# Stick-breaking attention layer on one core: a new split of the projection stream and a new order on ScalarE

## The chip, the cores and the metric

The kernel runs on one core of one Trainium2 chip. The metric is the device time of one execution in microseconds (us), lower is better.

## What is computed

The layer is one residual block, `x + mixer(rmsnorm(x))`, followed by a final RMSNorm, for 2048 tokens of 1024 channels in float32. The mixer projects to q, k, v and a gate g (`w_in`, 1024 x 4096), has 16 heads of 64 channels, multiplies the heads' output by silu(g) and projects back. Its attention is strictly causal:

```python
z = einsum(q[t], k[s]) / sqrt(64)
log_rem = where(s < t, log_sigmoid(-z), 0)
after = cumsum(log_rem, reversed over s) - log_rem
w = where(s < t, exp(log_sigmoid(z) + after), 0)
o = w @ v
```

## The kernel before

Tokens are reversed, so that the reversed cumulative sum becomes a forward scan. Every float32 operand is split into a high and a low part, and a product is three matmuls (high x high, high x low, low x high).

**Stages.** First v is projected and the input scaled (to about 200 us). Then comes the attention stage (about 232 to 1466 us), into which the projections of q, k and g are woven. Last come the gated output projection and the final norm (1466 us to the end).

**The attention stage** goes over heads h, chunks c of 512 query tokens and blocks j = c..3 of 512 key positions. One (h, c, j) is a *slot*: 160 slots, 10 in a head, in the order c0j0, c0j1, c0j2, c0j3, c1j1, ..., c3j3. A slot with j = c is *diagonal* and starts a chunk. A slot has two *halves* (320 halves) of two steps each (`STEPS`, L137). In each half

- TensorE turns two blocks of scanned rows into one pair of PSUM banks (`turns`, L890: up to 16 transposes of 64 rows), multiplies the turned rows of the half before with the value differences into the bank `o_ps` (`weigh_beside`, L969, twice: once for the lower and once for the upper 64 rows), and makes the scores of two steps of two slots further on (L865).
- ScalarE copies the turned rows to `r_turned_hi` (`hi`, L1182), takes the sigmoid of the two new scores (`stick`, L1175), and stores with its own DMA queue.
- VectorE subtracts to get `r_turned_lo` (`lo`, L1402) and runs two scans (`scan`, L1390).

There is one pair of turn banks only: `turns` of a half waits until `lo` of the half before is done (L893). There is one `o_ps` bank: the first weighing of a chunk waits until ScalarE has copied the finished chunk out (`empty`, L1186, wait at L953). Within `weigh_beside` the second weighing of a half waits until the last matmul of the first has finished (L976, L978), since both add into the same bank.

**Row halves.** All these matmuls use 64 of the 128 rows of the array. A matmul on the upper 64 rows and one on the lower 64 rows can run beside each other. While one row half weighs, the other makes scores.

**The stream.** The projections of q, k and g are 178 groups of 24 matmuls for each row half (`group_half`, L908; 256 columns each; 4272 for the upper rows and as many for the lower). They are the filling of the attention stage. `UPTO` (L169) says how many upper ones are to be done by the end of each half: 12 more in a half of a diagonal slot, 15 more in any other (`QUOTA`, L156). The lower rows stay 30 (`BEHIND`) behind. `weigh_beside` first lets the row half that has less to do take some stream matmuls; then `group_pairs` (L933) issues upper and lower ones in turn. Its last call in a half has `share` 1 and issues what is left, first uppers, then lowers.

```python
both = min(left(h, 0), left(h, 1)) // share
for _ in range(both):
    group_half(0)
    group_half(1)
```

**Finished groups.** When a group is complete, ScalarE copies its bank to `made` (`made_high`, L1135), VectorE makes the low part (`made_low`, L1377), and ScalarE issues the store of the high part (L1152) and of the low part (`store_low`, L1158), which waits for VectorE. ScalarE's order in a half (L1287 to L1316) is: copy and high store of finished groups, `hi`, `store_low`, two sigmoids, then in a diagonal slot `empty` (first half) or the two stores of the chunk (second half, L1192).

**The planner.** Which half finishes a group (`FINISHED`, L170) follows from `UPTO`, and from that the steps at which weights are loaded (`LOAD_W`, L176) and at which the last pieces are prepared (L202 to L213).

## Time and profile before

| | us |
|---|---|
| median of three runs | 1629.98 |
| lowest, highest | 1627.0, 1630.36 |
| the profiled execution, its own time | 1635.98 |
| its span, first to last instruction | 1634.2 |
| TensorE busy (matmuls) | 1573.5 |
| VectorE busy | 1282.4 |
| ScalarE busy | 883.9 |
| mean granted TensorE clock, share of full speed | 0.992 |

PE is TensorE (PEld its weight loads), DVE is VectorE, ACT is ScalarE, POOL is GpSimd; a q behind a name is the engine's sequencer, where it issues DMAs. A matmul's duration in the profile includes its way through the array: the distance between the starts of two that follow each other is shorter than a duration. A row of a timeline has start, length, engine, line, operation, output<-input, shapes and count, and in brackets the idle time before it with what ended it.

### The profile page before, as it was taken

How to read it: one execution, taken by the hardware profiler on the slowest of the kernel's cores; microseconds unless marked ns; L12 is line 12 of the kernel's file. 1: busy time of each engine (PE TensorE's matmuls, PEld its weight loads, DVE VectorE, ACT ScalarE, POOL GpSimd, SP SyncE). 2: the span in 40 equal slices, each digit the busy share in tenths (PEclk: the TensorE clock that was granted, in tenths of full speed). 3: DMA queues.
4: the chain of work that ended last, by engine and by line, in shares of the span. 5: the costliest groups of instructions: out<-in, count | busy, mean ns of one | idle time of the engine just before them, and what ended most of it. 6: DMA issues, size and time to landing. Idle time of an engine off the chain costs nothing. (4 is left out here: it accounts for less than half of the span.)

```text
span 1634.2 us, 46030 instructions
## 1 busy us (share of the span) xinstructions
PE 1573.5 (96%) x19314; PEld 1459.2 (89%) x19314; DVE 1282.4 (78%) x1525; ACT 883.9 (54%) x1558; POOL 414.0 (25%) x520
## 2 busy tenths in 40 slices
PE   9999989999999999999999999999999998999998
PEld 7888889899999999998999899999999998868887
DVE  4535338888888888897888898889889897967873
ACT  6635336566655666665655566656655665842221
POOL 0022033224323243323332433324422340000000
PEclk9999989999999999999999999999999999999999
DMA  9968643434334252434343343524253436779621
GB/s 306 274 180 272 183 142 109 124 111 124 124 105 122 88 156 76 140 94 129 105 121 115 111 118 102 152 73 140 81 157 87 123 102 204 249 248 318 203 103 65
DMA packets 205933, 238.57 MB, mean 146 GB/s; under 512 B 54560, under 2 KB 162080, under 8 KB 205728
## 3 DMA queue, kind: packets, MB, share of 16 engines
q1 hardware_dynamic: 113344, 160.30, 32.0%
q10 hardware_dynamic: 92384, 75.33, 15.2%
q8 instruction: 154, 2.52, 0.7%
q14 instruction: 51, 0.42, 0.1%
HBM read 155.78 MB, written 79.76 MB: 144 GB/s over the span
## 5 line engine op out<-in xcount | busy, mean ns | idle before, releaser
L957 PE MATMUL o_ps<-r_turned_hi,dv_head 64*128 64x512 f32 (+3 forms) x1280 | 481.4, 380 | 21.6 <-ACT o_stage L1190 19.7
L1400 DVE TENSOR_TENSOR_SCAN u<-u,u 128x512 f32<-128x512 f32 x384 | 485.5, 1304 | 0.0
L1179 ACT ACTIVATE u<-z_ps 128x512 f32<-128x512 f32 (+3 forms) x640 | 330.9, 533 | 265.1 <-PE z_ps L880 177.0
L923 PE MATMUL group_ps<-hT_hi,w_hi 64*128 64x256 f32 x1888 | 453.6, 281 | 2.9 <-DVE made L1384 2.0
L957 PE MATMUL o_ps<-r_turned_lo,dv_head 64*128 64x512 f32 (+3 forms) x1280 | 454.1, 365 | 0.0
L923 PE MATMUL group_ps<-hT_hi,w_lo 64*128 64x256 f32 x1888 | 448.8, 280 | 0.0
L923 PE MATMUL group_ps<-hT_lo,w_hi 64*128 64x256 f32 x1888 | 447.6, 279 | 0.0
L1404 DVE TENSOR_TENSOR r_turned_lo<-turn_ps,r_turned_hi 128x1024 fp32r<-128x1024 f32 (+1 forms) x320 | 337.5, 1055 | 130.6 <-ACT r_turned_hi L1184 129.8
L1184 ACT ACTIVATE r_turned_hi<-turn_ps 128x1024 fp32r<-128x1024 f32 (+1 forms) x320 | 287.5, 899 | 172.6 <-PE turn_ps L902 149.6
L923 PEld LDWEIGHTS group_ps<-hT_hi,w_hi 64*128 64x128 f32 x1888 | 318.5, 186 | 8.1 <-DVE made L1384 2.8
L923 PEld LDWEIGHTS group_ps<-hT_lo,w_hi 64*128 64x128 f32 x1888 | 314.4, 186 | 2.1
L923 PEld LDWEIGHTS group_ps<-hT_hi,w_lo 64*128 64x128 f32 x1888 | 314.0, 186 | 1.0
L957 PEld LDWEIGHTS o_ps<-r_turned_hi,dv_head 64*128 64x128 f32 x1280 | 240.8, 188 | 36.3 <-issue 31.1
L923 PE MATMUL z_ps<-hT_hi,w_hi 64*128 64x256 f32 x960 | 270.8, 282 | 0.7 <-DVE made L1384 0.4
L923 PE MATMUL z_ps<-hT_hi,w_lo 64*128 64x256 f32 x960 | 269.5, 281 | 0.0
L923 PE MATMUL z_ps<-hT_lo,w_hi 64*128 64x256 f32 x960 | 268.6, 280 | 0.0
L880 PE MATMUL z_ps<-k_hi_twice,q_hi 64*128 64x512 f32 (+3 forms) x640 | 260.7, 409 | 3.8 <-ACT u L1179 2.9
L957 PEld LDWEIGHTS o_ps<-r_turned_lo,dv_head 64*128 64x128 f32 x1280 | 240.0, 187 | 4.3
L756 POOL TENSOR_SCALAR w_raw<-w_raw,a_norm_col 128x128 f32<-128x128 f32 x192 | 165.3, 877 | 266.2 <-DMA w_raw<-in_w_qkg 266.2
L880 PE MATMUL z_ps<-k_hi_twice,q_lo 64*128 64x512 f32 (+3 forms) x640 | 232.2, 364 | 0.0
L880 PE MATMUL z_ps<-k_lo_twice,q_hi 64*128 64x512 f32 (+3 forms) x640 | 231.7, 364 | 0.0
L902 PE MATMUL turn_ps<-ident,u 64*128 64x64 f32 x4352 | 206.2, 224 | 23.4 <-DVE r_turned_lo L1404 22.7
(180 smaller groups left out, 3253.2 us busy)
## 6 DMA issues: line engine op xcount, KB each, us to landing
qk_hi_cols<-made ACTq DMA_DIRECT2D x128, 128.0 KB, 2.4
qk_lo_cols<-made ACTq DMA_DIRECT2D x128, 128.0 KB, 2.5
k_hi_twice<-qk_hi_cols SPq DMA_DIRECT2D x128, 128.0 KB, 3.2
k_lo_twice<-qk_lo_cols SPq DMA_DIRECT2D x128, 128.0 KB, 3.6
x_T<-in_xT SPq DMA_DIRECT2D x29, 512.0 KB, 6.5
w_raw<-in_w_qkg SPq DMA_DIRECT2D x24, 512.0 KB, 4.0
x_rows<-in_x SPq DMA_DIRECT2D x16, 512.0 KB, 4.8
v_rows<-v_stage ACTq DMA_DIRECT2D x32, 256.0 KB
```

The lines of the kernel that those rows point to most:

```text
L756: last = nc.gpsimd.tensor_scalar(w_raw[t % 2][:, k, :], w_raw[t % 2][:, k, :], norm_col[:, k:k + 1], None, ALU.mult)
L880: last = nc.tensor.matmul(score_bank(m), a[c % 2][rows, tau], b[rows, sig], start=(n == 0), stop=(n == 2))
L902: last = nc.tensor.transpose(turn_ps[:, half, at:at + HALF], u_t[m // CB % RU][t][rows, r * P - lo:(r + 1) * P - lo], ident[rows, rows])
L923: last = nc.tensor.matmul(bank_of(g)[:, 0:GW], a[t % 2][rows, k, :], b[rows, c // 2, k, cols], start=(n == 0 and not low), stop=(n == QPM ...
L957: last = nc.tensor.matmul(o_ps[:, 0:w], dv_head[rows, j * CB + sigma_block(m), :], turned_part[p % 2][rows, here], start=first, stop=(end ...
L1179: nc.scalar.activation(u_t[(m // CB) % RU][r][:, 0:w], score_bank(m), ACT.Sigmoid, scale=-Z_SCALE).then_inc(s_u, 1)
L1184: nc.scalar.activation(by_halves(rt_hi[p % 2][:], p), turned(p), ACT.Copy).then_inc(s_hi, 1)
L1400: nc.vector.tensor_tensor_scan(u, u, other, start, ALU.mult, op).then_inc(s_r, 1)
L1404: nc.vector.tensor_tensor(by_halves(rt_lo[p % 2][:], p), turned(p), by_halves(as_f32(rt_hi[p % 2][:]), p), ALU.subtract).then_inc(s_lo, 1)
```

## The change

The quotas 12 and 15 go. `limits` works out for each half how long VectorE's work would outlast TensorE's, averages this over three halves, adds an equal amount to each so that the sum fits, and caps a half at 16. The lower rows may come no nearer to the upper ones than 26. `group_pairs` takes a largest count in place of the share; in the second half of a diagonal slot it is also called ahead of the first weighing. ScalarE issues `store_low` behind both sigmoids, and `empty` comes between them. Three helper functions only move up in the file.

```diff
-QUOTA = {True: 12, False: 15}
+SWITCH = 4
+STREAM_HALVES = 2 * (NU - 4)
+MOST = 16
+SCAN_COLUMN, LOW_COLUMN = 5.8, 2.3
+
+def spare_columns(h):
+    s, p = h // 2, h
+    low = blocks_of_pair(p) * P
+    scans = [CH - score_cols(m) for m in range(PAIR * h + LEAD_SCORES - PAIR, PAIR * h + LEAD_SCORES) if m < NS]
+    scored = [CH - score_cols(m) for m in range(PAIR * h + LEAD_SCORES, PAIR * h + LEAD_SCORES + PAIR) if m < NS]
+    weighed = 2 * blocks_of_pair(max(p - 1, 0)) * P
+    return SCAN_COLUMN * sum(scans) + LOW_COLUMN * low - low - weighed - 1.5 * sum(scored)
 
 def limits():
-    upto = [0]
+    each = [spare_columns(h) / (GW + 10) for h in range(STREAM_HALVES)]
+    spare = [sum(each[max(h - 1, 0):h + 2]) / len(each[max(h - 1, 0):h + 2]) for h in range(STREAM_HALVES)]
+    more = (STREAM + BEHIND - sum(spare)) / STREAM_HALVES
+    upto, total = [0], 0.0
     for h in range(2 * NU):
-        _, c, j, _ = STEPS[CB * (h // 2)]
-        upto.append(min(upto[-1] + QUOTA[c == j], STREAM + BEHIND))
+        total += spare[h] + more if h < STREAM_HALVES else 0
+        upto.append(max(upto[-1], min(round(total), STREAM + BEHIND, upto[-1] + MOST)))
     return upto
...
                 def left(h, low):
                     limit = UPTO[h + 1] - BEHIND if low else UPTO[h + 1]
+                    if low and made_so_far[0] < STREAM:
+                        limit = min(limit, made_so_far[0] - QPM - 2)
                     return max(0, min(limit, STREAM) - made_so_far[low])
 
-                def group_pairs(h, share):
-                    both = min(left(h, 0), left(h, 1)) // share
-                    for _ in range(both):
+                def group_pairs(h, most=QPM):
+                    for _ in range(min(left(h, 0), left(h, 1), most)):
                         group_half(0)
                         group_half(1)
-                    if share == 1:
+                    if most == QPM:
                         for low in range(2):
                             for _ in range(left(h, low)):
                                 group_half(low)
...
-                    group_pairs(2 * s, 2)
+                    group_pairs(2 * s, SWITCH)
                     weigh_beside(2 * s - 1, 0, ahead + 1, 2 * s)
-                    group_pairs(2 * s, 1)
+                    group_pairs(2 * s)
...
                     turns(2 * s + 1)
+                    if diagonal(s):
+                        group_pairs(2 * s + 1, SWITCH)
                     weigh_beside(2 * s, 0, ahead + 2, 2 * s + 1)
-                    group_pairs(2 * s + 1, 2)
+                    group_pairs(2 * s + 1, SWITCH)
                     weigh_beside(2 * s, 1, ahead + 3, 2 * s + 1)
-                    group_pairs(2 * s + 1, 1)
+                    group_pairs(2 * s + 1)
...
                         if inside(s):
                             hi(h)
+                        if inside(s + LEAD):
+                            stick(first + LEAD_SCORES)
+                        if ended is not None and part == 0:
+                            empty(ended)
+                        if inside(s + LEAD):
+                            stick(first + LEAD_SCORES + 1)
                         for g in finished(h - 1):
                             store_low(g)
-                        if inside(s + LEAD):
-                            stick(first + LEAD_SCORES)
-                            stick(first + LEAD_SCORES + 1)
...
-                        if ended is not None and part == 0:
-                            empty(ended)
```

## Rows read from the trace of the kernel before

**Rows 1.** The page: busy time and share of the span of each engine.
```profile
PE 1573.5 (96%) x19314; PEld 1459.2 (89%) x19314; DVE 1282.4 (78%) x1525; ACT 883.9 (54%) x1558; POOL 414.0 (25%) x520
```

**Rows 2.** Who waited for whom, TensorE, 238 to 1466 us: total, times, longest.
```profile
PE turn_ps L902 <- DVE r_turned_lo L1404: 22.7, 41, 2.0
PE o_ps L957 <- ACT o_stage L1190: 19.7, 53, 3.7
```

**Rows 3.** Timeline of TensorE around 802 us: stream matmuls of both row halves.
```profile
802.04 0.27 PE L923 MATMUL group_ps<-hT_hi,w_hi 64*128 64x256 f32 x1
802.15 0.27 PE L923 MATMUL group_ps<-hT_lo,w_hi 64*128 64x256 f32 x1
802.18 0.28 PE L923 MATMUL z_ps<-hT_hi,w_hi 64*128 64x256 f32 x1
...
802.30 0.28 PE L923 MATMUL z_ps<-hT_lo,w_hi 64*128 64x256 f32 x1
```

**Rows 4.** Timeline of TensorE around 1420 us: stream matmuls of the lower half alone.
```profile
1419.71 0.28 PE L923 MATMUL z_ps<-hT_hi,w_lo 64*128 64x256 f32 x1
...
1420.78 0.28 PE L923 MATMUL z_ps<-hT_hi,w_lo 64*128 64x256 f32 x1
```

**Rows 5.** Timeline of TensorE at 248 us: upper stream matmuls alone, then transposes.
```profile
248.29 0.28 PE L923 MATMUL group_ps<-hT_hi,w_lo 64*128 64x256 f32 x1
248.41 0.28 PE L923 MATMUL group_ps<-hT_hi,w_hi 64*128 64x256 f32 x1
248.42 0.28 PE L902 MATMUL turn_ps<-ident,u 64*128 64x64 f32 x1
248.53 0.28 PE L923 MATMUL group_ps<-hT_lo,w_hi 64*128 64x256 f32 x1
248.54 0.27 PE L902 MATMUL turn_ps<-ident,u 64*128 64x64 f32 x1
248.66 0.28 PE L923 MATMUL group_ps<-hT_hi,w_lo 64*128 64x256 f32 x1
248.66 0.46 PE L902 MATMUL turn_ps<-ident,u 64*128 64x64 f32 x5
```

**Rows 6.** Timeline of TensorE at 1423 us: the end of one weighing and the next.
```profile
1423.08 0.39 PE L957 MATMUL o_ps<-r_turned_lo,dv_head 64*128 64x512 f32 x1
1423.10 0.28 PE L923 MATMUL z_ps<-hT_hi,w_hi 64*128 64x256 f32 x1
1423.22 0.28 PE L923 MATMUL z_ps<-hT_lo,w_hi 64*128 64x256 f32 x1
1423.61 0.46 PE L957 MATMUL o_ps<-r_turned_hi,dv_head 64*128 64x512 f32 x1
```

**Rows 7.** Timeline of ScalarE, first half of a slot that starts a chunk.
```profile
840.90 0.60 ACT L1179 ACTIVATE u<-z_ps 128x512 f32<-128x512 f32 x1 [0.86 <-PE z_ps L880]
841.39 0.59 ACT L1190 ACTIVATE o_stage<-o_ps 128x512 f32<-128x512 f32 x1
```

**Rows 8.** The same moment on TensorE.
```profile
841.47 0.39 PE L902 MATMUL turn_ps<-ident,u 64*128 64x64 f32 x6
842.13 0.47 PE L957 MATMUL o_ps<-r_turned_hi,dv_head 64*128 64x512 f32 x1 [0.27 <-ACT o_stage L1190]
```

**Rows 9.** ScalarE's waits that the moved operations touch, 238 to 1466 us.
```profile
ACT u L1179 <- DVE made L1386: 43.1, 52, 1.9
ACT u L1179 <- DVE made L1384: 37.6, 40, 1.8
ACT o_stage L1190 <- DMA o_lo_cols<-o_stage: 4.0, 3, 3.1
```

**Rows 10.** The low store's issue on ScalarE's queue: ns min/median/max, first and last start.
```profile
L1161 ACTq DMA_DIRECT2D qk_lo_cols<-made x128: 326/327/1886, 188.8 to 1262.7; - x128
L1161 ACTq DMA_DIRECT2D gate_cols<-made x64: 321/326/364, 483.1 to 1427.5; - x64
```

**Rows 11.** Timeline of ScalarE between a chunk's stores and the next turned rows.
```profile
851.47 1.65 ACTq L1196 DMA_DIRECT2D o_hi_cols<-o_stage  x1
851.78 0.59 ACT L1179 ACTIVATE u<-z_ps 128x512 f32<-128x512 f32 x1
853.15 0.61 ACTq L1197 DMA_DIRECT2D o_lo_cols<-o_stage  x1
853.87 0.42 ACT L1127 ACTIVATE dv_head<-v_here 128x256 fp32r<-128x256 f32 x1 [1.49 <-issue]
854.19 1.01 ACT L1184 ACTIVATE r_turned_hi<-turn_ps 128x1024 fp32r<-128x1024 f32 x1
```

**Rows 12.** Timeline of VectorE over one half of a non-diagonal slot.
```profile
858.74 0.40 DVE L1386 TENSOR_TENSOR made<-group_ps,made 128x256 fp32r<-128x256 f32 x1
859.05 1.22 DVE L1404 TENSOR_TENSOR r_turned_lo<-turn_ps,r_turned_hi 128x1024 fp32r<-128x1024 f32 x1
860.18 2.46 DVE L1400 TENSOR_TENSOR_SCAN u<-u,u 128x512 f32<-128x512 f32 x2
```

More of the change, by code:

```diff
@@ L155, with score_cols, sigma_block, turn_width @@
 BEHIND = 30
-QUOTA = {True: 12, False: 15}
-STREAM = (NG - FIRST) * QPM
+SWITCH = 4
+def score_cols(m):
+    _, c, j, r = STEPS[m]
+    return r * P if j == c else 0
+def sigma_block(m):
+    _, c, j, r = STEPS[m]
+    return CB - 1 - r if j == c else r
+def turn_width(m):
+    _, c, j, _ = STEPS[m]
+    return (sigma_block(m) + 1) * P if j == c else CH
+def blocks_of_pair(p):
+    return (turn_width(PAIR * p) + turn_width(PAIR * p + 1)) // P
+STREAM = (NG - FIRST) * QPM
+STREAM_HALVES = 2 * (NU - 4)
[8 more added lines that the diff above has]
+    return SCAN_COLUMN * sum(scans) + LOW_COLUMN * low - low - weighed - 1.5 * sum(scored)
 def limits():
-    upto = [0]
+    each = [spare_columns(h) / (GW + 10) for h in range(STREAM_HALVES)]
+    spare = [sum(each[max(h - 1, 0):h + 2]) / len(each[max(h - 1, 0):h + 2]) for h in range(STREAM_HALVES)]
+    more = (STREAM + BEHIND - sum(spare)) / STREAM_HALVES
+    upto, total = [0], 0.0
     for h in range(2 * NU):
-        _, c, j, _ = STEPS[CB * (h // 2)]
-        upto.append(min(upto[-1] + QUOTA[c == j], STREAM + BEHIND))
+        total += spare[h] + more if h < STREAM_HALVES else 0
+        upto.append(max(upto[-1], min(round(total), STREAM + BEHIND, upto[-1] + MOST)))
     return upto
@@ L213 @@
 LAST_SLOT = LAST_PIECE_STEP // CB
-def score_cols(m):
-    _, c, j, r = STEPS[m]
-    return r * P if j == c else 0
-def sigma_block(m):
-    _, c, j, r = STEPS[m]
-    return CB - 1 - r if j == c else r
-def turn_width(m):
-    _, c, j, _ = STEPS[m]
-    return (sigma_block(m) + 1) * P if j == c else CH
 def chunk_end(u):
@@ L239, in blocks_before @@
     return turn_width(m - 1) // P if m % PAIR else 0
-def blocks_of_pair(p):
-    return (turn_width(PAIR * p) + turn_width(PAIR * p + 1)) // P
 def inside(u):
@@ L499, in lows_stored, with diagonal @@
                 eng.wait_ge(s_gst[parity], low_stores(g, parity))
+        def diagonal(u):
+            return STEPS[CB * u][1] == STEPS[CB * u][2]
         def score_bank(m):
```

## The prediction

> **What bounds the kernel.** I read the page's busy line first: TensorE is busy 96% of the span, VectorE 78%, ScalarE 54% [rows 1]. So the change can gain only what TensorE waits, or lose by making TensorE's own work longer. Next come TensorE's waits over the attention stage [rows 2]: 22.7 us in 41 waits of transposes for VectorE's `r_turned_lo`, and 19.7 us in 53 waits of a chunk's first weighing for ScalarE's copy of `o_ps`. No other wait there is above 2 us. A stream matmul lasts 0.28 us in the profile but the next on its row half starts 0.118 us after it, so a wait hides about another 0.16 us behind the last matmul's tail: 41 x 0.16 = 6.6 and 53 x 0.16 = 8.5 us. The two waits are worth about 29 and 28 us.
>
> The third view is the timeline of TensorE, for what a stream matmul costs. Where uppers and lowers are issued in turn, each row half starts one about every 0.12 us, both halves at once (802.04, 802.15 on one bank, 802.18, 802.30 on the other) [rows 3]. Where only one row half has work, the distance is the same: from 1419.71 to 1420.78 there are ten starts, so nine distances of 0.118 [rows 4]. **A single costs as much as a pair.** So what matters is in which order uppers and lowers are issued.
>
> **Part 1, the order of the stream.** The new `left` holds the lower rows 26 behind the uppers. At the end of a half they are 30 behind. When the last `group_pairs` of a half starts, the uppers still have the rest of the half's quota to go, so `left(h, 1)` is at most 4 or so, and `range(min(...))` is worked out once, before the loop. It issues those few pairs; what is left then follows in the two loops below: all uppers, then all lowers. Before the change `min(left, left)` gave the full rest, and at most two were left single in the steady halves. I counted this out of the code for all 320 halves: after the change 258 halves end in a run of n uppers followed by at least n lowers (n from 1 to 12, most often 8), together 1271 pairs that are no longer issued in turn. Before there are none.
>
> What this costs depends on how far one row half may run ahead of the other. The trace shows it where the first halves have uppers only [rows 5]. All transposes stand behind the stream matmuls in the program. Yet one starts at 248.42, right behind the stream matmul of 248.41, with those of 248.53 and 248.66 still to come, and the first transpose, of the upper rows, as well: it has passed three matmuls. The next start at 248.54 and 248.66, in step with the stream, while transposes otherwise follow each other closer (six of them in 0.39 us) [rows 8]. So a matmul passes three that wait on the other row half and no more. Then the lowers of a run of n start with the (n-3)rd upper, (n-4) x 0.118 us later than in turn. Over the 258 halves the sum of n-4, where positive, is 381: 381 x 0.118 = **+45 us**.
>
> The bounds: nothing, if the limit of three is not general (0), and 1013 x 0.118 = 120 us if a lower could start only with the last upper. I take 45, since rows 5 are the only place with exactly this pattern.
>
> The Trainium skill ("TensorE: Matmul & The Clock Gate", Step-by-step: what each phase is for) says that only weight loads are pulled ahead and the matmuls themselves stay in program order, in a window 64 deep. The trace disagrees: the transpose at 248.42 started before two stream matmuls that precede it. By that rule the term would be the 120 us.
>
> **Part 2, fewer pairs between the two weighings.** The second weighing of a half waits for the end of the first (L976, L978). In the tail, where few stream matmuls are left, the last weighing matmul starts at 1423.08 and the next weighing at 1423.61: 0.54 us is the least distance [rows 6]. Before, 5 to 9 stream matmuls of the same row half lie between them in the steady halves, at least 0.22 + 4 x 0.118 = 0.7 us: no wait. After, `SWITCH` and the limit of 26 leave fewer. By the count, in the second halves of c0j2, c1j2, c2j2 and c2j3 (61 halves) none is left for the row half that weighed: it has 0.22 us of work and idles 0.31 us. In those of c0j1, c0j3 and c1j3 (47 halves) two are left: 0.22 + 0.24, idle 0.08. 61 x 0.31 + 47 x 0.08 = **+23 us**. The bounds are 0, if the other row half's work covers it, and 108 x 0.31 = 33 us.
>
> **Part 3, the copy of `o_ps` earlier, and four pairs ahead of the chunk's first weighing.** Before, the copy stands behind the second sigmoid: that starts at 840.90, the copy at 841.39, and the weighing at 842.13 after 0.27 us idle [rows 7, 8]. Put between the sigmoids, the copy comes 0.49 us earlier, and four pairs (0.47 us) move ahead of the weighing. Together 0.96 us against a mean wait of 19.7 / 53 + 0.16 = 0.53 us. It takes away all but the long ones that come from the landing of the chunk before (4.0 us in 3) [rows 9]: 28 - 4 = **-24 us**. The work moved is the same, so nothing is added. The second sigmoid starts some 0.5 us later; its scan is a half later. What is late next is the copy of turned rows, `hi`: it still starts behind the same sum of ScalarE's work.
>
> **Part 4, the new shares.** Per half they become about 16 in c0j0 to c0j2, 15 to 16 in c1j1 and c1j2, 11 to 12 in c0j3, c1j3 and c3j3, and 8 in the second half of c2j3, in place of 12 and 15. The stream's sum is unchanged, so the shares cost nothing by themselves; they decide which waits go. The waits of the transposes lie in the first halves of c0j0, c0j1, c0j2, c1j1, c1j2 and c2j3. There the chain copy 1.01, `lo` 1.22 [rows 11, 12] starts late, since ScalarE has two stores and `dv_hi` ahead of it [rows 11]. All but c2j3 get longer by parts 1 and 4 (0.4 to 0.9 us a slot), more than their mean wait. I take two thirds of 29: **-20 us**. Bounds: 0 and -29. In return VectorE needs 1.22 + 2.46 and 0.40 where a group ends, 3.7 to 4.1 us [rows 12], in the second halves of c0j3 and c1j3, where TensorE's work shrinks to about 3.5 us; the next half is long and takes it up. Free.
>
> **Part 5, `store_low` behind the sigmoids.** The sigmoids waited 43.1 + 37.6 us for VectorE's low part [rows 9], but TensorE hardly waited for a sigmoid (not in rows 2), so that by itself gives nothing. The issue of 0.33 us [rows 10], 178 times, moves from time in which ScalarE waited to the stretch right before the next `hi`. In c2j3, which does not get longer, and for the chunk stores' halves it delays `lo`: about half of 16 x 0.33 = 2.6, **+3 us**; bounds 0 and 20 (a third of the 178, each in full). The transfers start under 2 us later and are needed slots later. POOL and SP queues see only shifts of one or two halves in the loads (`LOAD_W` follows `FINISHED`): free, covered by a lag of 9 steps; if that cover went, a group's first matmul would wait.
>
> **Sum.** 45 + 23 - 24 - 20 + 3 = **+27 us**, against the profiled execution's own 1635.98: 1663. This execution is 6.0 us above the median of the runs, so the forecast is 1657 us. I lean a little to the gain's side, since restarts after each of the 94 waits of before also fall away, and say **1654**.
>
> **The rivals.**
> - *Runs cost nothing, the waits go* (faster). Place: the join of uppers and lowers. If the lowers may pass eight or more waiting uppers, part 1 is 0 and the sum is -18; without part 2 as well it is -41. It decides from a reach of seven on. That gives 1612 (1589 to 1612), chance 0.17. For it: the sequencer runs far ahead, and nothing in steady halves before shows a limit. Against it: rows 5.
> - *In balance.* Reach of five to six, 20 us less than forecast and a little more of the waits: 1627 to 1633. Chance 0.08.
> - *The waits stay* (parts 1, 2 and 5 in full, half of 3 and 4): 1630 + 71 - 22 = 1679, with part 5 at its upper end 1690. For it: ScalarE's stores ahead of `hi` are not shortened. Chance 0.17.
> - *Strict program order*: 120 in place of 45, 1729. Rows 5 speak against it. The page of the skill named above is for it. Chance 0.03.
> - *The change does what its words say*, pairs ahead and shares by VectorE with the rest in turn: this is the first rival; the count of the code excludes it but for the reach.
>
> The forecast's own case (1634 to 1679) has 0.55. A measurement of this kernel can tell 0.2%, 3.3 us, from no change. So slower by over 0.2%: 0.55 + 0.17 + 0.03 = 0.75; within: 0.08; faster: 0.17. The range leaves 0.1 on either side: 1612 to 1690. The forecast's own range is 1634 to 1679.
>
> **What would show it.** Right: runs of 5 to 8 stream matmuls 0.12 us apart on one bank at the ends of halves, the other row half idle until three are left; more time in c0j0 to c0j2, less in c0j3 and c1j3; TensorE's wait for `o_stage` under 4 us; the turns' wait near 8 us. TensorE's busy time stays high or grows, for a run on one row half counts as busy. Part 2 shows as gaps of 0.1 to 0.3 us before a weighing with no releaser but TensorE itself. Wrong: lowers that start with the first upper of a run; or waits for `r_turned_lo` as large as before.

## The result, and the profile after

The changed kernel takes 1676.43 us (median of four runs, 1675.84 to 1689.57) against 1630.17 for the kernel before, a ratio of 1.030 (95% interval 1.0245 to 1.0357). It is slower by 49 us, where 24 were forecast. The profiled execution is the longest of the four, 1689.57 us. All sums below are made from the ratios, as 1628 x (ratio - 1), 1628 being what the kernel before takes in most of the comparisons. A difference of two such ratios is uncertain by 4 to 11 us, which is given where it matters. One execution in this study, of the kernel with four stream matmuls moved back, was in a slower state (2685.72 us at a granted clock of 0.59) and is left out of that kernel's figures.

The page of the changed kernel, busy time of each engine:

```profile
PE 1652.0 (98%) x19314; PEld 1545.4 (92%) x19314; DVE 1290.3 (76%) x1525; ACT 885.0 (52%) x1558; POOL 406.5 (24%) x520
```

TensorE has the same 19314 matmuls as before [rows 1] and is busy 78.5 us longer with them, the other engines are not. Its waits, 238 to 1466 us (total, times, longest):

```profile
PE turn_ps L921 <- DVE r_turned_lo L1427: 7.1, 11, 1.5
PE o_ps L977 <- ACT o_stage L1212: 3.9, 2, 3.7
```

Both waits of [rows 2] are all but gone: 42.4 us have become 11.0. And still the kernel is slower. TensorE's busy time in the steady part, from 250 us to the last half of the stream, first after, then before (a row has the stretch, its length, TensorE's busy time with the number of matmuls, the granted clock, the DMA share and GB/s):

```profile
250.00:1468.00 1218.00, 1199.62 (x16980) 1.00 0.40 118
```

```profile
250.00:1422.00 1172.00, 1127.06 (x16981) 1.00 0.41 122
```

Idle time falls from 44.9 to 18.4 us, busy time grows by 72.6 us. The granted clock is 1.00 in both rows (the full level, 2.4 GHz), and the matmuls are the same, so what has changed is how well they lie beside each other. The timeline of TensorE at the end of a half (c0j1, second half) shows it:

```profile
805.52 0.28 PE L942 MATMUL group_ps<-hT_hi,w_hi 64*128 64x256 f32 x1
805.56 0.28 PE L942 MATMUL z_ps<-hT_hi,w_hi 64*128 64x256 f32 x1
805.64 0.28 PE L942 MATMUL group_ps<-hT_lo,w_hi 64*128 64x256 f32 x1
...
806.12 0.28 PE L942 MATMUL group_ps<-hT_hi,w_lo 64*128 64x256 f32 x1
806.13 0.38 PE L942 MATMUL z_ps<-hT_lo,w_hi 64*128 64x256 f32 x1
806.25 0.28 PE L942 MATMUL group_ps<-hT_hi,w_hi 64*128 64x256 f32 x1
806.35 0.28 PE L942 MATMUL z_ps<-hT_hi,w_lo 64*128 64x256 f32 x1
806.37 0.28 PE L942 MATMUL group_ps<-hT_lo,w_hi 64*128 64x256 f32 x1
806.47 0.28 PE L942 MATMUL z_ps<-hT_hi,w_hi 64*128 64x256 f32 x1
806.49 0.28 PE L942 MATMUL group_ps<-hT_hi,w_lo 64*128 64x256 f32 x1
```

This is a run of eight. The uppers write `group_ps`, 0.12 us apart: five from 805.64 to 806.12 and three more to 806.49; the lowers write `z_ps`. The last lower in turn starts at 805.56 and the next at 806.13, with the fifth upper of the run: three uppers are still to come. That is the reach of three which [rows 5] gave, in a steady half.

Outside the steady part the clock is not always full: at the start of the attention stage it is at its half level (1.2 GHz) for 10.2 us before the change and for 13.7 us after it, and in the last head for 20.4 us after it against 10.2 before. That is part of the 1689.57 us, and it returns below.

The second part shows in the second half of c0j2, where no stream matmul is left between the two weighings for the row half that weighed:

```profile
812.57 0.39 PE L977 MATMUL o_ps<-r_turned_lo,dv_head 64*128 64x512 f32 x1
812.65 0.28 PE L942 MATMUL group_ps<-hT_hi,w_hi 64*128 64x256 f32 x1
812.77 0.28 PE L942 MATMUL group_ps<-hT_lo,w_hi 64*128 64x256 f32 x1
813.06 0.46 PE L977 MATMUL o_ps<-r_turned_hi,dv_head 64*128 64x512 f32 x1
813.06 0.32 PE L899 MATMUL z_ps<-k_hi_twice,q_hi 64*128 64x128 f32 x1
```

The distance from the last matmul of the first weighing to the next weighing is 0.49 us (0.54 in [rows 6]), and the score behind it, on the row half that is free, starts no earlier than the weighing.

The sigmoids' waits for VectorE [rows 9] have left ScalarE's list; the sigmoids now wait for their scores. The wait for the landing of the chunk before is longer, since the copy is asked for earlier (238 to 1520 us; in the window of [rows 9] it is 10.0 us against 4.0):

```profile
ACT u L1201 <- PE z_ps L899: 146.6, 253, 1.8
...
ACT o_stage L1212 <- DMA o_lo_cols<-o_stage: 15.6, 11, 5.6
```

### The profile page after: what moved, and what is told of

The parts are those of the page before. It is cut to its first block, busy times and chain, and to the rows that moved or that the text cites. A ratio compares the mean times of both kernels' runs of the same rounds, so it can differ in the third digit from the quotient of the medians.

```text
span 1687.8 us, 46030 instructions
## 1 busy us (share of the span) xinstructions
PE 1652.0 (98%) x19314; PEld 1545.4 (92%) x19314; DVE 1290.3 (76%) x1525; ACT 885.0 (52%) x1558; POOL 406.5 (24%) x520
## 4 chain that ended last, share of the span: by engine, by line
PE 62%; DVE 2%; DMA 2%; ACT 2%; ACTq 1%; issue 1%; SPq 0%; POOL 0%; DVEq 0%
PE group_ps L942 16%; PE o_ps L977 14%; PE z_ps L899 9%; PE z_ps L942 8%; PE turn_ps L921 6%; PE z_ps L1034 4%; PE turn_ps L1034 3%; PE group_ps L1034 2%; DVE u L1423 1%; PE o_ps L1034 1%; DVE r_turned_lo L1427 1%; DMA o_lo_cols<-o_stage 1%; ACT r_turned_hi L1206 1%; ACTq L1218 0%; DMA w_raw<-in_w_qkg 0%
## 5 line engine op out<-in xcount | busy, mean ns | idle before, releaser
L977 PE MATMUL o_ps<-r_turned_hi,dv_head 64*128 64x512 f32 (+3 forms) x1280 | 491.1, 388 | 8.3 <-ACT o_stage L1212 3.9
L942 PE MATMUL group_ps<-hT_hi,w_hi 64*128 64x256 f32 x1888 | 467.8, 283 | 1.1 <-DVE made L1409 0.9
L942 PE MATMUL group_ps<-hT_hi,w_lo 64*128 64x256 f32 x1888 | 467.3, 283 | 0.0
L942 PE MATMUL group_ps<-hT_lo,w_hi 64*128 64x256 f32 x1888 | 466.8, 283 | 0.0
L942 PEld LDWEIGHTS group_ps<-hT_hi,w_lo 64*128 64x128 f32 x1888 | 319.6, 186 | 0.7
L942 PEld LDWEIGHTS group_ps<-hT_lo,w_hi 64*128 64x128 f32 x1888 | 319.0, 186 | 0.7
L899 PE MATMUL z_ps<-k_hi_twice,q_hi 64*128 64x512 f32 (+3 forms) x640 | 273.8, 431 | 4.1 <-ACT u L1201 2.6
L942 PE MATMUL z_ps<-hT_lo,w_hi 64*128 64x256 f32 x960 | 273.9, 285 | 0.0
L921 PE MATMUL turn_ps<-ident,u 64*128 64x64 f32 x4352 | 249.5, 228 | 12.6 <-DVE r_turned_lo L1427 12.2
L921 PEld LDWEIGHTS turn_ps<-ident,u 64*128 64x128 f32 x4352 | 227.0, 139 | 20.3 <-DVE r_turned_lo L1427 14.0
```

What stands on the lines that cost most here:

```text
L899: last = nc.tensor.matmul(score_bank(m), a[c % 2][rows, tau], b[rows, sig], start=(n == 0), stop=(n == 2))
L921: last = nc.tensor.transpose(turn_ps[:, half, at:at + HALF], u_t[m // CB % RU][t][rows, r * P - lo:(r + 1) * P - lo], ident[rows, rows])
L942: last = nc.tensor.matmul(bank_of(g)[:, 0:GW], a[t % 2][rows, k, :], b[rows, c // 2, k, cols], start=(n == 0 and not low), stop=(n == QPM ...
L977: last = nc.tensor.matmul(o_ps[:, 0:w], dv_head[rows, j * CB + sigma_block(m), :], turned_part[p % 2][rows, here], start=first, stop=(end ...
```

## The experiments

There were fourteen. The first question was what each part does, by taking parts out of the changed kernel and by adding one part to the kernel before. Later ones ask why the shares brought nothing and why runs cost less than worked out.

### The runs

**All in turn.** The changed kernel, with its last loops in turn:

```diff
                     if most == QPM:
-                        for low in range(2):
-                            for _ in range(left(h, low)):
-                                group_half(low)
+                        while left(h, 0) or left(h, 1):
+                            for low in range(2):
+                                if left(h, low):
+                                    group_half(low)
```

> The changed kernel, with the last stream matmuls of each half issued in turn (one upper, one lower) in place of all uppers and then all lowers; shares, bounds, ScalarE's order and the pairs ahead of the weighing as in the changed kernel. Theory (a lower may pass three waiting uppers, so a run of n costs (n-4) x 0.118 us): 45 us less than the changed kernel's 1676, 1631 us. If the runs cost more than I worked out and make up the whole miss of 22 us, 1609. Rival (runs cost nothing, the time went into the waits between the two weighings and the smaller shares): 1676. Rival (strict program order): 1676 - 120 = 1556.

Measured: 1.0116 of the kernel before (1.0077 to 1.0155), median 1648.2. The runs cost 1.0301 - 1.0116, that is **30 us** (19 to 41) where 45 were forecast. Runs that cost nothing are excluded, and so is strict program order.

These 30 us contain a difference of the clock. The mean granted clock of the four executions is 0.989 here and 0.992 in the changed kernel. Among the executions of the kernel before, 0.001 of mean clock goes with 1.2 to 1.5 us (in one comparison 1622.58 us at 0.997 and 1636.9 us at 0.990), so by this estimate the runs cost some 4 us more than 30 at the same clock. Heads 2 to 15 of the two profiled executions, all at the full level, say the same (the table below): 34.6 us of 41 worked out.

**Runs alone, in the kernel before.** The pairs of the last call of each half are put apart:

```diff
                     both = min(left(h, 0), left(h, 1)) // share
-                    for _ in range(both):
+                    apart = min(both, 24) if share == 1 else 0
+                    for _ in range(both - apart):
                         group_half(0)
                         group_half(1)
+                    for low in range(2):
+                        for _ in range(apart):
+                            group_half(low)
```

> The kernel before, with the pairs of the last call of each half (4 to 7, 1706 in all) issued as n uppers and then n lowers; nothing else changed. Theory (reach of three): the sum of n-4 is 492, x 0.118 = 58 us, so 1688. Rival (strict program order, n-1 each, 1398): 165 us, 1795. Rival (runs cost nothing): 1630.

> As the one with all pairs apart, but only the last four pairs of each half (1214 in all). Theory (reach of three: the lowers start with the first upper of the run but the order of the two row halves after it is the same): 0, 1630, at most some 5 us more. Rival (strict program order, 906 x 0.118): 107 us, 1737. Rival (any run costs by its length, whatever the reach, as 58 x 1214/1706): 41 us, 1671.

Measured: all apart 1.0194 (1.0148 to 1.024), +32 us; at most four apart (24 replaced by 4) 1.0044 (1.0021 to 1.0067), +7 us. The shape is that of a reach of three: 492 units of n-4 cost 32 us, 1214 pairs in runs of at most four cost 7. By a price for any run as long as it is, the second would have been 32 x 1214 / 1706 = 23. The size is off, though: 32 against 58, and 1658 us against the 1688 expected.

**Runs in second halves only** (`if share == 1 and h % 2`), and **runs in a kernel that waits little** (the 1601 us kernel with shares by hand, told of further down, with all its last pairs apart):

> The kernel before with the pairs of the last call apart (n uppers, then n lowers) in second halves only. The same in all halves cost 30 us where 58 were expected, with 19 us less idle time of TensorE: a run costs (n-4) x 0.118 only where the transposes behind it would not have waited for VectorE. Theory: the sum of n-4 over second halves is 231, x 0.118 = 27 us; the transposes behind those halves are first halves', where most of the 22.7 us of waits are, so about half of it is hidden: 1640 to 1645. Rival (the cost lies in the halves themselves and nothing is hidden): 1655. Rival (second halves carry none of it): 1630.

> The fastest kernel so far (ScalarE's new order and nine shares per head moved by hand to the halves with waits, 1601 us; its transposes wait 11.9 us and its weighing for the output bank 7.5, against 22.7 and 19.7 in the kernel before) with the pairs of each half's last call apart, as in the second of these kernels. The sum of n-4 is the same as there, 492, gross 58 us. Theory (a run costs nothing where TensorE would have waited anyway): there 30 us net were paid and 19 us of idle time went; here only about 9 can go, so 58 - 9 = 49 less what was short there too (58 - 49): 40 us, 1641. Rival (a run simply costs half of what was worked out, waits or not): 30 us, 1631.

Measured: second halves 1.0122 (1.0075 to 1.0169), +20 us of 27 worked out, where the theory had 10 to 15 and the rival 25. The other one 0.9983 against 0.9806 without the runs: +29 us (22 to 36). There my theory of the waits forecast 40 and the rival, half the price in any case, 30. Yet waits did go there, as the two lists of TensorE's waits show, without the runs and with them:

```profile
PE turn_ps L902 <- DVE r_turned_lo L1405: 11.9, 23, 1.3
PE o_ps L957 <- ACT o_stage L1190: 7.5, 5, 3.9
```

```profile
PE o_ps L961 <- ACT o_stage L1194: 5.8, 7, 3.0
PE turn_ps L902 <- DVE r_turned_lo L1409: 5.1, 10, 1.1
```

Set beside each other, over the same work in each: from the first transpose of the second head to the first of the last head, 14 heads, by the profiles. In this order the rows are the kernel before, the same with all runs, with runs in second halves, the kernel with few waits without and with runs, the changed kernel in turn, and the changed kernel:

```profile
313.93:1372.35 1058.42, 1022.94 (x15460) 1.00 0.40 116
306.81:1391.62 1084.81, 1065.40 (x15461) 1.00 0.39 113
316.56:1395.98 1079.42, 1051.60 (x15461) 1.00 0.39 114
303.93:1336.81 1032.88, 1016.06 (x15460) 1.00 0.41 119
312.93:1370.72 1057.79, 1050.21 (x15461) 1.00 0.40 116
305.03:1369.39 1064.36, 1042.03 (x15420) 1.00 0.40 114
315.82:1414.79 1098.97, 1087.36 (x15421) 1.00 0.38 110
```

| runs in | worked out for these heads, gross | busy, more | idle, less | length, more |
|---|---|---|---|---|
| kernel before, all | 53 | 42.5 | 16.1 | 26.4 |
| kernel before, second halves | 25 | 28.7 | 7.7 | 21.0 |
| kernel with few waits | 53 | 34.2 | 9.2 | 24.9 |
| changed kernel | 41 | 45.3 | 10.7 | 34.6 |

These are single executions, and one differs from another by some 5 us here: 1051.24 and 1056.12 us in two kernels that differ only in the last head. Between a quarter and two fifths of what busy time grows by is paid out of time in which TensorE would have stood idle. In the changed kernel, and with runs in second halves only, the growth is about the gross price or a little more; with runs in all halves 10 and 19 us of the gross price don't appear at all.

Where it is paid shows when each class of half is taken by itself, in the kernel before with all apart, as the change of the half that follows (medians over 14 heads). With n = 7, where (n-4) x 0.118 = 0.35 us: +0.24 behind c0j1's second half, +0.27 and +0.33 behind the first and second half of c0j3, +0.27 and +0.47 behind those of c1j3. With n = 6 (0.24 us) it is +0.32 behind c1j1's second half, but 0.00, -0.01, -0.03 and -0.02 behind the first halves of c0j1, c0j2, c1j2 and c2j3, and +0.01 behind c0j0's second. Behind the last of these TensorE had waits to give, 0.33 us on average. Behind the first halves of c0j1, c0j2, c1j2 and c2j3 it had none, or 0.03 us in c1j2, and why a run is free there was not settled. These four are the first halves in which the uppers have one or two stream matmuls over (c0j2, c1j2, c2j3) or three beside the second weighing (c0j1), so the uppers may already have been the longer side; that was not tried.

### Few stream matmuls between the weighings

**Four pairs everywhere.** The changed kernel, with `left` asked anew for each pair:

```diff
-                    for _ in range(min(left(h, 0), left(h, 1), most)):
-                        group_half(0)
-                        group_half(1)
-                    if most == QPM:
-                        for low in range(2):
-                            for _ in range(left(h, low)):
-                                group_half(low)
+                    for _ in range(most):
+                        for low in range(2):
+                            if left(h, low):
+                                group_half(low)
```

> The changed kernel with every call of group_pairs worked out anew at each pair, so that all stream matmuls go in turn (as in the first of these kernels) and four pairs, not one or two, lie between the two weighings of a half and ahead of a diagonal slot's second half. Shares, the limit of 26 and ScalarE's order as in the changed kernel. Theory (part 2: the second weighing waits for the first, with too few stream matmuls between): the 23 us of part 2 go from the 1648 of the first kernel, 1625. Rival (the new shares themselves hold the rest): 1645 to 1648.

**None**, in the kernel before:

```diff
-                    group_pairs(2 * s, 2)
...
-                    group_pairs(2 * s + 1, 2)
```

> The kernel before without the call of group_pairs between the two weighings: its pairs go to the end of the half, in turn as all others. Between the weighings stay only the 0 to 4 stream matmuls that weigh_beside puts there. Theory (part 2: 0.31 us idle in each half where the first weighing's row half has nothing, 0.08 where it has two, nothing with three or more): by the count of those, at most 308 x 0.31 = 95 us more, 1660 to 1725. Rival (the other row half's scores and the work queued behind cover it): 1630 to 1640.

Measured: 1.0025 (1.0009 to 1.004), median 1630.9, where 1625 was expected, so 1.0116 - 1.0025 = **15 us** (8 to 22) for part 2, and 1.0335 (1.0309 to 1.0362), +55 us, for none. The first gives the place too. Between these two versions the second halves of c0j2, c1j2 and c2j2, three of the four classes for which the count had found nothing, differ by 0.41, 0.36 and 0.40 us, c2j3's by 0.16 (0.31 forecast for each), and those with two left, c0j1, c0j3 and c1j3, by 0.11, 0.08 and 0.12 (0.08 forecast). These seven classes together are 1.65 us a head, 23 us in heads 2 to 15. All classes together are 0.94 us a head, 13 us: the rest comes back where TensorE had waited for VectorE, above all in c2j3's first half (0.45 us shorter, 0.56 us less idle). So part 2 has its full size, and filled waits give back some two fifths of it. The same moment as above, with four pairs, has the weighing 0.49 us behind as before, and stream matmuls all the way to it and beyond:

```profile
781.84 0.39 PE L974 MATMUL o_ps<-r_turned_lo,dv_head 64*128 64x512 f32 x1
781.84 0.28 PE L942 MATMUL group_ps<-hT_hi,w_lo 64*128 64x256 f32 x1
...
782.30 0.28 PE L942 MATMUL group_ps<-hT_hi,w_hi 64*128 64x256 f32 x1
782.33 0.46 PE L974 MATMUL o_ps<-r_turned_hi,dv_head 64*128 64x512 f32 x1
```

### ScalarE's order and the pairs ahead

**The order alone**, in the kernel before (`store_low` behind the sigmoids, `empty` between them, as in the diff of the change), and **the order with the new calls of `group_pairs`**, old shares, no limit of 26:

> The kernel before with ScalarE's new order alone: the copy of the output bank between the two sigmoids, the store of the low part behind both. Theory: the copy comes 0.49 us earlier against a mean wait of 0.53 us, so some 20 of the 28 us of the wait for the output bank go; the later store costs 3: 1630 - 17 = 1613. Rival (the store pushes the next copy of turned rows): 1630 or more, with a larger wait for r_turned_lo. Rival (what is late next is the turned rows anyway, the wait only moves): 1625 to 1630.

> The kernel before with ScalarE's new order and the new calls of group_pairs (four pairs between the weighings and four ahead of a diagonal slot's second half), with the old shares and without the limit of 26, so that no runs arise. Theory (the ScalarE order has already taken the waits for the output bank, and four pairs cover the distance between the weighings): as with ScalarE's order alone, 1616, within 4. Rival (the pairs ahead of the weighing are what helps): under 1608. Rival (four between the weighings are too few where the old kernel had up to nine): 1625 or more.

Measured: 0.993 (0.9903 to 0.9957), **-11 us**, and 0.9927 (0.9904 to 0.995), -12 us. TensorE's waits with the order alone:

```profile
PE turn_ps L902 <- DVE r_turned_lo L1405: 21.4, 40, 1.7
PE o_ps L957 <- ACT o_stage L1190: 5.8, 3, 3.9
```

Of 19.7 us of visible waits for the output bank [rows 2] 13.9 are gone, 50 of 53, and the time fell by 11 (7 to 16). In heads 2 to 15 idle time fell by 12.9 us and the length by 13.1. So a wait was worth what the list shows of it, and no more shows: the 0.16 us each that I had added for matmuls' tails (8.5 us) are not seen. The new calls, pairs ahead of the weighing and four between, together change nothing that can be told beside the order (0.9927 and 0.993, uncertain by 6 us).

### The shares

**The new shares with the order**, old calls, all in turn (`limits` and the limit of 26 as in the change, `left` asked anew for each pair):

> The kernel before with ScalarE's new order and the new shares; half of what is left goes between the weighings as before; the limit of 26 is in, but worked out anew at each pair, so that all go in turn. Theory (part 4: the shares take waits for r_turned_lo away and cost nothing): 8 to 20 us under ScalarE's order alone, 1596 to 1608. Rival (TensorE gets longer halves where it was not late and shorter ones where VectorE then is late): 1616 or more, with more idle time in c0j3, c1j3 and c2j3.

Measured: 0.9977 (0.9957 to 0.9997), so +8 us (2 to 13) on the order alone, the rival's side. With the new calls it is 1.0025 (four pairs, new shares) against 0.9927 (old shares), **+16 us** (12 to 20). TensorE's waits with the new shares and the old calls:

```profile
PE turn_ps L938 <- DVE r_turned_lo L1445: 18.7, 30, 2.9
PE o_ps L997 <- ACT o_stage L1230: 8.1, 6, 4.6
```

18.7 in place of 21.4: the shares by themselves take away next to nothing. With the new calls (old shares and new shares compared, by class of half) 0.50 us of idle time go from c0j0's first half and 0.20 from c0j1's, and 0.33 come to c0j0's second half, 0.38 to c2j3's first, 0.12 to its second and 0.09 to c1j3's first. The waits moved, in part to where the shares are smallest.

Where the 16 us lie shows when the two profiled executions are cut at the same work: 6 us in heads 2 to 15 (1051.24 against 1044.92, with idle time up by 5.1), 6 us in the last head (91.16 against 85.39 up to the last transposes), 3 us before head 2 (the version with the new shares has 6.8 us at the half level there, the other none), 1 us at the end. The clock is part of it: the mean is 0.990 in the ten executions with the new shares and 0.994 in the four with the old, some 5 us by the estimate above. For the old calls the same cut gives 4 us in heads 2 to 15, which is within the 5 us of one execution against another, and 5 us in the last head.

**Four stream matmuls moved back**, from c0j0's second half to c2j3:

```diff
+    for h in range(HS // CB * 2 * (H - 1)):
+        at = h % (HS // CB * 2)
+        upto[h + 1] -= 4 if 1 <= at < 16 else 1 if at == 16 else 0
     return upto
```

> The changed kernel with all stream matmuls in turn, as two kernels ago (1631), and four of the 16 of c0j0's second half moved to c2j3: three to its first half, one to its second. Theory (the new shares leave c2j3's first half too short, TensorE waits 0.90 us there on average, 0.5 more than before, for r_turned_lo): 3 x 0.118 = 0.35 us of that wait goes in each of 15 heads, 1631 - 5 to 8 = 1623 to 1626. Rival (the place doesn't matter, only the sum): 1631.

Measured: 1.0003 (0.9972 to 1.0034; median 1631.7), against 1.0025 without: no difference that can be told, where 5 to 8 us were expected. c0j0's second half became 0.60 us shorter, as it should, c2j3's two halves 0.29 and 0.11 longer, but its wait fell only from 0.90 to 0.74, and 0.15 and 0.13 us of idle time came to the first halves of c0j0 and c0j1. I expected the wait of the half that gets longer to go. It mostly didn't.

**Shares by hand.** Old quotas, nine per head moved to the first halves whose transposes wait:

```diff
-QUOTA = {True: 12, False: 15}
+QUOTA = {(0, 0): (15, 12), (0, 1): (17, 15), (0, 2): (15, 14), (0, 3): (14, 13), (1, 1): (12, 12), (1, 2): (17, 15), (1, 3): (14, 13), (2, 2): (12, 12), (2, 3): (17, 13), (3, 3): (12, 12)}
...
-        upto.append(min(upto[-1] + QUOTA[c == j], STREAM + BEHIND))
+        upto.append(min(upto[-1] + QUOTA[c, j][h % 2], STREAM + BEHIND))
```

> The kernel before with ScalarE's new order, and of the old shares nine per head moved to the halves in which the transposes wait: c0j0 15, 12; c0j1 17, 15; c1j2 17, 15; c2j3 17, 13; c0j2 15, 14; c0j3 and c1j3 14, 13. The sum is the old one. Theory (a wait for r_turned_lo goes where its own half gets longer, and a half without a wait can be shortened for nothing): 9 x 0.118 x 16 = 17 us at most of 1616, some 10 of them, so 1606. Rival (the waits only move to the shortened halves, as with the new shares): 1613 to 1624.

> The kernel before with ScalarE's new order, the new calls of group_pairs and shares fitted to that kernel's waits (c0j0 17, 12; c0j1 19, 15; c1j2 18, 15; c2j3 18, 12; c0j2 15, 14; c0j3 and c1j3 13, 12; c3j3 12, 11). Its transposes wait 35.5 us, more than without the new calls, with the same time. Theory (as before, with more to take): 15 per head moved, x 0.118 x 16 = 28 us at most, some 16, so 1600. Rival (the waits only move): 1613 to 1624.

Measured: with the old calls 0.9806 (0.9768 to 0.9844), median **1601.0 us**, the fastest kernel of this study, 32 us under the kernel before and 20 (13 to 28) under ScalarE's order alone, where 10 were expected and 17 at most; its list of waits is above, 11.9 us where the order alone has 21.4. With the new calls and a stronger table 0.9913 (0.988 to 0.9946), -14 us, no better than without any table (-12): the waits for `r_turned_lo` fall from 35.5 to 24.9, and c0j1's second half gets 0.51 us idle instead. So shares can take the waits: small steps with the old calls did, large ones with the new calls mostly moved them. Which of the two differences decides was not tried.

**The last head.** The new planner puts the first pieces of the output's columns (`o_part_hi`, `gated_hi`) four steps later and the copies of the output weights' high part (`wo_hi`) two steps later. In the version with four pairs everywhere this is ScalarE at the end (ACTq its DMA issues), with the turns that wait:

```profile
1405.25 0.61 ACTq L1216 DMA_DIRECT2D o_lo_cols<-o_stage  x1
1405.48 0.66 PE L921 MATMUL turn_ps<-ident,u 64*128 64x64 f32 x16
1405.91 1.28 ACT L1228 ACTIVATE o_part_hi<-o_part_hi,v_first_T 128x128 f32<-128x128 f32 x4 [0.59 <-issue]
1407.10 1.05 ACT L1190 ACTIVATE wo_hi<-wo_raw 128x1024 fp32r<-128x1024 f32 x1
1408.04 0.61 ACT L1234 ACTIVATE gated_hi<-o_part_hi 128x512 fp32r<-128x512 f32 x1
1408.56 1.04 ACT L1190 ACTIVATE wo_hi<-wo_raw 128x1024 fp32r<-128x1024 f32 x1
1409.51 0.36 ACT L1161 ACTIVATE made<-group_ps 128x256 f32<-128x256 f32 x1
1409.77 1.00 ACT L1203 ACTIVATE r_turned_hi<-turn_ps 128x1024 fp32r<-128x1024 f32 x1
1410.81 1.22 DVE L1424 TENSOR_TENSOR r_turned_lo<-turn_ps,r_turned_hi 128x1024 fp32r<-128x1024 f32 x1 [0.48 <-ACT r_turned_hi L1203]
1412.09 1.11 PE L921 MATMUL turn_ps<-ident,u 64*128 64x64 f32 x16 [3.02 <-DVE r_turned_lo L1424]
```

The transposes end at 1406.14, the copy of their rows starts at 1409.77, and TensorE stands 3.02 us. The changed kernel has the same at 1468.65, 2.66 us, and the kernel before has no wait there above 1.0 us. In the experiment the copies of `wo_hi` go elsewhere:

```diff
-WO_HIGH_AT = {WO_FROM[k // (KT // 2)] + 6 + k // (KT // 2) + 2 * (k % (KT // 2)): k for k in range(KT)}
+WO_HIGH_AT = {WO_FROM[k // (KT // 2)] + 5 + 3 * (k // (KT // 2)) + 2 * (k % (KT // 2)): k for k in range(KT)}
```

> The changed kernel with all stream matmuls in turn and four between the weighings (1631), and the eight copies of the output weights' high part (wo_hi, 1.05 us each on ScalarE) at other steps of the last head: none in the half right after a chunk's stores, where the new planner put two of them and where TensorE then waits 3.0 us for r_turned_lo. Theory (a planner shift of four steps brings 4 us of ScalarE's work together ahead of one copy of turned rows): that wait falls from 3.0 to about 1 us and the clock's half level behind it goes or shrinks; 2 to 5 us in all, 1626 to 1629. Rival (the wait comes from the stores and the pieces of the first output columns alone): the wait stays over 2 us and the time 1631.

Measured: 0.9971 (0.995 to 0.9992), against 1.0025: -9 us by the ratios, -6 by the medians (1625.1). The same moment:

```profile
1406.58 0.36 ACT L1161 ACTIVATE made<-group_ps 128x256 f32<-128x256 f32 x1
1406.84 1.01 ACT L1203 ACTIVATE r_turned_hi<-turn_ps 128x1024 fp32r<-128x1024 f32 x1
...
1409.17 0.52 PE L921 MATMUL turn_ps<-ident,u 64*128 64x64 f32 x10 [1.14 <-DVE r_turned_lo L1424]
```

The wait is 1.14 us, and the half and the next one take 4.73 and 3.91 us in place of 6.61 and 4.55. The next one is shorter because of the clock, first without, then with the copies moved:

```profile
1412.09:1416.64 4.55, 4.55 (x43) 0.68 0.06 17
```

```profile
1409.17:1413.08 3.91, 3.90 (x46) 1.00 0.52 170
```

Without the move the granted clock is at its half level from 1411.5 to 1414.9, from the end of the 3.02 us in which TensorE stood; with it the clock stays full, as the expectation had it. In the changed kernel and in its version in turn the half level at the same wait lasts 10.2 us. The last head as a whole is 4.5 us shorter (86.67 against 91.16 up to the last transposes). The rest of the 6 to 9 us is not located, but the mean clock of the twelve executions is 0.994 against 0.990 of the ten, so less time at the half level is a likely part of it, argued from these figures and not tested by itself.

## Why the prediction was right or wrong

The direction was right, and the runs and the gaps cost time where they were sought. The size was not: +27 us forecast (24 after my own discount), +49 measured. Term by term, with the experiments put in a row, so that the measured terms add up by the way they are made:

| part | forecast | measured | from |
|---|---|---|---|
| runs (part 1) | +45 | +30 | 1.0301 - 1.0116 |
| few between the weighings (part 2) | +23 | +15 | 1.0116 - 1.0025 |
| new shares and limit, all in turn (part 4) | -20 | +16 | 1.0025 - 0.9927 |
| ScalarE's order and pairs ahead (parts 3, 5) | -21 | -12 | 0.9927 |
| sum | +27 | +49 | 1.0301 |

**Part 1** held in mechanism: the reach of three is in the timeline, runs of four cost less than a quarter of what all cost, and strict program order, which would have given 1556 for the version in turn and 1737 and 1795 for the runs in the kernel before, is out. The Trainium skill ("TensorE: Matmul & The Clock Gate", Step-by-step: what each phase is for) says that matmuls stay in program order. For matmuls on different row halves the traces disagree (806.13 and [rows 5]). By the ratios the term measured two thirds of its size, by heads 2 to 15 more (34.6 us of 41), with 10.7 us of the growth taken from idle time.

**Part 2** held, with its places: six of the seven classes of half that the count named show the 0.31 and 0.08 us to within 0.1; in c2j3 it is half. Together they have the 23 us, but 10 us came back from waits that the gaps filled. What I had not seen is that the score queued behind the waiting weighing is held as well, on either row half, so only work ahead of it in the program covers this wait.

**Part 3** held in mechanism and was too large: with the order alone the visible 19.7 us went but for 5.8, and gave 11, about what they showed. The step of this part that failed is "a wait hides about another 0.16 us behind the last matmul's tail". It made 28 of 20 and 29 of 23. Without it part 3 is -16.

**Part 4 is the step that failed**, by 36 us. "I take two thirds of 29: -20 us" rested on "All but c2j3 get longer by parts 1 and 4 (0.4 to 0.9 us a slot), more than their mean wait". The waits did go, as forecast, from 22.7 to 7.1 us. But they went because the gaps and the runs of parts 2 and 1 filled them (33.5 us with neither, 13.8 with the gaps, 7.1 with both), and a wait that is filled with a loss is no gain. The version with all in turn and four between has the new shares alone, and its waits for `r_turned_lo` are 33.5 us, hardly less than the 35.5 of the same calls with the old shares. In my sum the idle time was credited to the shares, and parts 1 and 2 were charged in full as if none of it paid for them. The other sentence that failed is "TensorE's work shrinks to about 3.5 us; the next half is long and takes it up. Free": with shares of 8 to 12, c2j3 and c1j3's first half took on idle time. And of the shifts in the planner I looked only at SP's and POOL's loads; the pieces on ScalarE, two and four steps later in the last head, met a chunk's stores. Moving one kind of them gave 6 to 9 us (uncertain by 4), and the profiles show 6 of the 16 us in the last head. The forecast had no term for the clock; it stands in part 4's measured term with some 5 us by estimate. Part 4 is off by +36 us, parts 1 and 2 by -15 and -8, parts 3 and 5 by +9: together the 22 us of the miss.

Of the rivals none came out. The range's upper end was mis-added: part 5 at its own upper bound gives 1679 + 17 = 1696, not 1690. The rival nearest, "the waits stay", has the right time (1679) for a reason that is not so: the waits are gone.

## What to carry to other kernels

Where two streams share an engine's array, the order of issue is part of the cost: a loop whose count is fixed before it starts can put all of one side ahead of the other and cost 2%. An engine that is busy 96% has 4% to gain from its waits, and each microsecond of them may be claimed once: a wait that a loss has filled can't be counted as a gain as well. Its busy time is no floor either: here the same matmuls took 72.6 us more when they lay less well beside each other. When a planner's quotas move, list everything that is derived from them on every queue, and find the moment at which two shifted pieces meet. And when two kernels are compared by a single profile, cut both at the same work and read the granted clock beside the time.

## What the runs showed of the hardware

A matmul on one row half starts ahead of at most three that precede it in the program and wait for the other row half; the timelines at 806.13 and [rows 5] show it, and the costs of runs of four (+7 us) and of all (+32 us) fit it in shape. This differs from a matmul that waits for a semaphore: the second weighing at 813.06 held back the score behind it, on the free row half, to the same instant. And a pair of weighings on one bank has a distance of 0.49 to 0.54 us from the last matmul of one to the first of the next, in which TensorE needs other work for both row halves: with only the 0 to 4 stream matmuls of `weigh_beside` there, 308 halves cost 55 us, 0.18 each. The granted clock goes down to its half level at the end of waits of 2.66 and 3.02 us in the last head (at 1467.8 for 10.2 us in the changed kernel, at 1411.5 for 3.4 us with four between) and stays full where the wait is 1.14 us. At the half level a matmul of 256 columns starts 0.21 us after the one before (from 1413.75 with four between), at the full level 0.118.
